# Entry of the attention's heads around two gate tiles, a second accumulator for the modulation, and the scan's last squares inside an output tile

## The chip, the core and the metric

One core of a Trainium2 chip runs one program: two blocks of a model at batch 1, 512 tokens, width 1024. TensorE multiplies matrices into PSUM (eight banks of 128 x 512 fp32 values), VectorE (DVE) and ScalarE (ACT) do elementwise work and functions, GpSimd (POOL) does elementwise work in SBUF, and SyncE (SP) issues DMAs. Every engine works through its own list of instructions in order and waits on semaphores. The metric is the time of one execution in microseconds; lower is better.

## What is computed

The stretch that the change touches lies in the first block. Cut to what matters:

```
mod = silu(c) @ w_ada + b_ada                    # six pieces of 1024: shift1, scale1, gate1, shift2, ...
h = rms_norm(x, norm1_w) * (1 + scale1) + shift1
q, k, v, xBC, z, dt_raw, gates = split(h @ w_in)
q, k = rms_norm per head, then axial rope
attn = softmax(q k^T / 8) v                      # 16 heads of 64, 4 kv heads, not causal
ssd = rms_norm((scan forward + scan backward + D x) * silu(z), ssd_norm_w)
merged = sigmoid(gates_a) * (attn @ w_attn_out) + sigmoid(gates_s) * (ssd @ w_ssd_out)
x = x + gate1 * (merged @ w_o)
```

All products are fp32 accurate. The second block (a recurrent layer and a latent attention) follows unchanged.

## The kernel before

**Tiles.** Activations lie feature by token, 512 tokens wide. A feature tile (`feature_tile`, L1032) is 128 output features: for each of 8 input blocks (4 for an output tile of the scan, `so`) three matmuls of 512 columns, high x high, high x low and low x high part, all into one PSUM bank; 24 matmuls (L1028 to L1030). With `mid=` a function is called on TensorE after half of the blocks.

**Weights.** They stream as 459 slabs of four blocks in the order of `plan()` (L105), two slabs for a tile of 8 blocks. SP loads a slab into one of 4 `w_raw` buffers, ScalarE copies the high part into one of 7 `w_hi` buffers (L592), GpSimd subtracts for `w_lo` (L550). `hi_upto(s)` stands in ScalarE's list wherever the conversion of slabs up to s is to be done, `AHEAD` = 6 slabs ahead of the tile in hand. A w_raw buffer is refilled once its w_lo is done, a w_hi buffer once the tile using it is done. GpSimd also does the rotary products of tile j (`rotate`, L540 and L541) at a fixed slab, seven behind the tile's own.

**Banks.** Each tile has a PSUM bank by its place in the order (L190 to L197): scan tiles from banks 0, 1, 7, the q, k, v tiles and late early-gate tiles from 0 and 1. It starts when the bank's last user has been read. Banks 0 and 1 serve the heads too: `ROW` (row of the negated maxima) is bank 0, `OQ` banks 7 and 1, `PST` (norm sums and statistics) and `OT` bank 2, `M` 3 and 4, `S` 5 and 6, `ADA` 7.

**End of the scan.** After the 16th pair TensorE does `stat("ssd", 15)` (L1195): four matmuls of one column over `sq_sum`, which holds the sum of earlier squares, then four over the last square from ScalarE. Then the last 8 output tiles, `("so", 3, m)`; block k of these needs `bL` of pair 12 + k.

**Projections.** Tiles k0, q0, k1, four value tiles, q1 to q7. A tile's statistic (`qk_stat`, one matmul of 512 columns) stands in the middle of the next tile. ScalarE: square, copy to `t[j % 2]` (L724) once tile j-2 is roped, root (`qk_root`, L734). VectorE per tile: shuffle (L1736), reciprocal of 512 columns (L1746), sum (L1741), product (L1775). Six tiles `("ga", m)` of the attention gate are done early, ScalarE taking their tanh into `gates_early` (L637): ga4 comes after q6, ga5 after q7.

**Heads.** For each head: two-part scores (L1241, L1242) of four key chunks alternate with the next head's scores for the maxima (L1221); VectorE takes the maxima (L1809), TensorE turns them into a row (`row_of_max`, L1229), ScalarE writes this into the 65th row of `q_lo` (L755), so that scores come out less their maximum; exponentials (L770); probabilities x values (L1250). Head 0's own maxima have no head to hide in: scores for maxima (0,0) and (0,1) follow q5, (0,2) and (0,3) follow ga4. After ga5 TensorE waits until all v tiles, q6, q7, ga4 and ga5 are evacuated, then does head 0's row, the q7 statistic and head 0.

**Modulation.** The 24 weight pieces of `w_ada` (2048 wide) are multiplied by silu(c) and added on VectorE (`ada_add`), 8 pieces for each third of the result; TensorE sums over partitions (`ada_reduce`: 16 matmuls of one column, L1098), VectorE takes the result (`ada_finish`). Thirds 2 and 3 run in the loop over m that merges gates and projections (tiles ga, gs, wa; two pieces per step), both in one buffer `acc2`. Third 2 is complete at the end of step m = 3 and is reduced after wa of step m = 4; third 3 is reduced amid the `wo` tiles. ScalarE issues the loads of the pieces (L781), each after the addition that frees its buffer; they stand in its list between the w_hi copies.

Of the kernel before, what the change touches and what calls it, by code (L numbers as in the profile page):

```python
# [9 lines left out]
ACT = mybir.ActivationFunctionType  # L10
# [52 lines left out]
EARLY_IN_QK = {("q", QT - 2): 4, ("q", QT - 1): 5}  # L63
# [127 lines left out]
for _name in TILES:  # L191
    _early = _name[0] == "ga" and _name[1] < N_EARLY
    _ring = (0, 1, 7) if _name[0] in MIXER or _early and _name[1] not in EARLY_IN_QK.values() else \
        (0, 1) if _name[0] in NARROW or _early else \
# [38 lines left out]

LAST_TILE = {}
# [20 lines left out]
def build(nc, d):  # L255

    with ExitStack() as ctx:
# [50 lines left out]
        with Arena():  # L308
# [32 lines left out]
            with Arena():  # L341
                cH, cL = sb("c_hi", [P, KT, SEQ], F32R), sb("c_lo", [P, KT, SEQ], F32R)
                piece2 = [sb(f"ada2_piece{b}", [P, ADA_W]) for b in range(2)]
                acc2 = sb("ada2_acc", [P, ADA_W])
# [235 lines left out]
        def _(act):  # L580
# [154 lines left out]

            for n, name in enumerate(QK):
                hi_upto(slab_of(name) + AHEAD)
                if n and n != KVT + 1:
                    qk_root(QK[n - 1])
                qk_copy(name)  # L740
                if name in EARLY_IN_QK:
                    gate_early(("ga", EARLY_IN_QK[name]))
# [10 lines left out]
            def max_row(h):  # L753
                act.wait_ge(rows_done, h + 1)
                A(qL[h % Q_RING][HD:HD + 1, :], ROW[0:1, :], ACT.Copy, scale=-1.0).then_inc(row_ready, 1)  # L755

# [4 lines left out]
            max_row(0)  # L761
            qk_root(QK[-1])
            hi_upto(slab_of(("gs", 0)) + AHEAD)
            for h in range(N_Q):
                for c in range(NCH):
                    n = NCH * h + c
                    act.wait_ge(qk_done, n + 1)
                    if h:
                        act.wait_ge(pv_done, n - NCH + 1)
                    A(PT[:, c, :], S[n % 2][:, :], ACT.Exp, scale=HD ** -0.5).then_inc(exp_done, 1)  # L770
# [236 lines left out]
        def _(pe):  # L1007
# [121 lines left out]
            def mixer_tile(name):  # L1129
# [4 lines left out]
                feature_tile(name, lambda k: bH[:, half + k, :], lambda k: bL[:, half + k, :], (rdyB, PPG * name[1]))  # L1134
# [60 lines left out]
            stat("ssd", PAIRS - 1)  # L1195
            for m in range(KT):
                mixer_tile(("so", N_GROUPS - 1, m))
# [63 lines left out]

            for n, name in enumerate(QK):
                feature_tile(name, in_a, in_a_lo, mid=(lambda: qk_stat(QK[n - 1])) if n and n != KVT + 1 else None)
                if n == 0:
                    rows("ssd")
                if n == KVT:
                    value_tiles()
                if name == ("q", QT - 3):
                    pe.wait_ge(y_ev, PAIRS)
                    for i in range(2):  # L1270
                        scores_for_max(0, i)
                if name in EARLY_IN_QK:
                    feature_tile(("ga", EARLY_IN_QK[name]), in_a, in_a_lo)
                if name == ("q", QT - 2):
                    for i in range(2, NCH):
                        scores_for_max(0, i)
# [1009 lines left out]
```

## Time and profile before

| | us |
|---|---|
| median of 3 runs | 1741.84 |
| lowest, highest run | 1740.32, 1755.98 |
| profiled execution | 1750.95 |
| its span, first to last instruction | 1749.2 |
| TensorE busy in the span | 1653.6 |
| VectorE, ScalarE, GpSimd busy | 1016.8, 743.0, 777.1 |
| mean granted TensorE clock | 0.969 |

The page of the profile gives busy time per engine, the chain of work that ended last, and groups of instructions by source line. TensorE's busy time includes the pipelined ends of its matmuls, so that it says little about small gaps; the timeline's idle times say more. The granted clock is 1.00 at 2.4 GHz and 0.50 at 1.2 GHz.

### The profile page before, as it was taken

What the parts mean: (1) busy time and instruction counts of PE and PEld (TensorE: products, weight loads), DVE (VectorE), ACT (ScalarE), POOL (GpSimd) and SP (SyncE); (2) the same over time, 40 slices, a digit from 0 to 9 for tenths busy, and PEclk for the clock granted to TensorE, in tenths of its full rate; (3) what the DMA queues carried; (4) which work ended last, traced back from release to release, by engine and by line L of the source; (5) the groups of instructions that cost most, each with busy time, mean ns of one, the idle gap of its engine ahead of it and who ended that gap; (6) DMA issues with size and microseconds to landing.
All of it is one profiled execution on the core that took longest, in us unless ns stands there. A gap on an engine that the chain in (4) does not pass through costs nothing.

```text
span 1749.2 us, 24032 instructions
## 1 busy us (share of the span) xinstructions
PE 1653.6 (95%) x8428; PEld 1365.8 (78%) x8428; DVE 1016.8 (58%) x1357; ACT 743.0 (42%) x1351; POOL 777.1 (44%) x548
## 2 busy tenths in 40 slices
PE   4899999999999899989989999999998799899998
PEld 4678888888787688878868888888887687677776
DVE  4778988988549497576241312122588624357652
ACT  2366655666434444222242323234566344323322
POOL 1245555656546310356534444445534363234433
PEclk9999999999999899989999999999999899799998
DMA  7243344334322100476323333333322232111211
GB/s 297 61 133 106 109 121 133 116 107 117 104 83 73 48 25 1 139 245 232 107 73 99 94 103 91 102 92 96 93 82 79 78 101 75 42 49 55 61 35 68
DMA packets 76390, 171.58 MB, mean 98 GB/s; under 512 B 8256, under 2 KB 8640, under 8 KB 72960
## 3 DMA queue, kind: packets, MB, share of 16 engines
q1 hardware_dynamic: 69120, 133.62, 25.9%
q10 hardware_dynamic: 7168, 36.57, 5.9%
q8 instruction: 68, 1.11, 0.3%
q14 instruction: 34, 0.28, 0.1%
HBM read 167.93 MB, written 2.23 MB: 97 GB/s over the span
## 4 chain that ended last, share of the span: by engine, by line
PE 80%; DVE 12%; ACT 3%; issue 2%; DMA 1%; POOL 0%; SPq 0%; DVEq 0%; ACTq 0%; POOLq 0%
PE bank L1028 21%; PE bank L1030 21%; PE bank L1029 21%; PE bank L1250 3%; DVE rstd L1746 1%; PE bank L1060 1%; PE bank L1430 1%; PE bank L1098 1%; PE bank L1184 1%; DMA x_stream<-x 1%; PE bank L1241 1%; DVE tmp L1593 1%; PE bank L1242 1%; PE bank L1192 1%; PE bank L1221 1%
## 5 line engine op out<-in xcount | busy, mean ns | idle before, releaser
L550 POOL TENSOR_TENSOR w_lo<-w_raw,w_hi 128x512 fp32r<-128x512 f32 x459 | 685.2, 1514 | 696.4 <-ACT w_hi L592 696.3
L1028 PE MATMUL bank<-a_hi,w_hi 128*128 128x512 f32 x1040 | 418.7, 403 | 16.6 <-DVE a_lo L1532 7.9
L1029 PE MATMUL bank<-a_lo,w_hi 128*128 128x512 f32 x1040 | 408.6, 393 | 0.0
L1030 PE MATMUL bank<-a_hi,w_lo 128*128 128x512 f32 x1040 | 408.3, 393 | 0.0
L592 ACT ACTIVATE w_hi<-w_raw 128x512 fp32r<-128x512 f32 x459 | 263.1, 620 | 161.9 <-PE bank L1030 137.6
L1028 PEld LDWEIGHTS bank<-a_hi,w_hi 128*128 128x128 f32 x1040 | 197.2, 190 | 68.4 <-issue 15.6
L1028 PE MATMUL bank<-b_hi,w_hi 128*128 128x512 f32 x600 | 237.9, 396 | 0.6 <-POOL w_lo L550 0.6
L1030 PE MATMUL bank<-b_hi,w_lo 128*128 128x512 f32 x600 | 236.0, 393 | 0.0
L1029 PE MATMUL bank<-b_lo,w_hi 128*128 128x512 f32 x600 | 235.9, 393 | 0.0
L1030 PEld LDWEIGHTS bank<-a_hi,w_lo 128*128 128x128 f32 x1040 | 197.4, 190 | 42.6
L1029 PEld LDWEIGHTS bank<-a_lo,w_hi 128*128 128x128 f32 x1040 | 197.8, 190 | 41.0 <-issue 1.9
L1028 PEld LDWEIGHTS bank<-b_hi,w_hi 128*128 128x128 f32 x600 | 114.4, 191 | 24.7 <-POOL w_lo L550 1.0
L1030 PEld LDWEIGHTS bank<-b_hi,w_lo 128*128 128x128 f32 x600 | 114.0, 190 | 24.6
L1029 PEld LDWEIGHTS bank<-b_lo,w_hi 128*128 128x128 f32 x600 | 114.2, 190 | 23.7
L1917 DVE SCALAR_TENSOR_TENSOR x_stream<-bank,small,x_stream 128x512 f32<-128x512 f32 x32 | 24.0, 751 | 140.4 <-PE bank L1030 140.4
L1910 DVE TENSOR_TENSOR tmp<-tmp 128x512 f32<-128x512 f32 x32 | 22.7, 708 | 123.5 <-ACT tmp L819 123.5
L690 ACT ACTIVATE M<-cs_rows,cs 128x128 f32<-128x128 f32 x256 | 78.0, 389 | 0.0
L1593 DVE SCALAR_TENSOR_TENSOR tmp<-bank,small,tmp 128x510 f32<-128x510 f32 (+1 forms) x96 | 72.0, 750 | 3.4
L504 POOL TENSOR_TENSOR square_sum<-square_sum,sq 128x512 f32<-128x512 f32 x31 | 40.1, 1292 | 64.6 <-ACT sq L604 64.6
L1508 DVE SCALAR_TENSOR_TENSOR ada_acc<-ada_piece,small,ada_acc 128x2048 f32<-128x2048 f32 x21 | 61.9, 2948 | 7.9 <-DMA ada_piece<-ada 6.1
L1250 PEld LDWEIGHTS bank<-v_and_ones,probs 128*128 128x128 f32 x512 | 63.7, 201 | 0.9
L1250 PE MATMUL bank<-v_and_ones,probs 128*128 128x65 f32 x512 | 63.8, 280 | 0.0
(328 smaller groups left out, 2500.9 us busy)
## 6 DMA issues: line engine op xcount, KB each, us to landing
w_raw<-ws SPq DMA_DIRECT2D x459, 256.0 KB, 2.7
cs_rows<-cs_scratch ACTq DMA_DIRECT2D x16, 1024.0 KB, 5.2
ada_piece<-ada ACTq DMA_DIRECT2D x16, 1024.0 KB, 5.7
ada_piece<-ada SPq DMA_DIRECT2D x8, 1024.0 KB, 14.9
x_stream<-x SPq DMA_DIRECT2D x1, 2048.0 KB, 16.2
x_stream<-x ACTq DMA_DIRECT2D x1, 2048.0 KB, 8.4
out<-x_stream SPq DMA_DIRECT2D x8, 256.0 KB, 2.2
rope_table<-rope ACTq DMA_DIRECT2D x1, 512.0 KB, 4.4
```

Of the source, the lines that this page charges most:

```text
L504: nc.gpsimd.tensor_tensor(sq_sum[:, :], first[:, :], sq[n % 2][:, :], ALU.add).then_inc(sq_added, 1)
L550: nc.gpsimd.tensor_tensor(wlo[b][:, :], raw[n % RAW_RING][:, :], r32(whi[b][:, :]), ALU.subtract)\
L592: A(whi[n % RING][:, :], raw[n % RAW_RING][:, :], ACT.Copy).then_inc(hi_done, 1)
L690: a(A(Dm[:, r, w], csB[:, r, w], ACT.Abs, bias=csT[:, c, h:h + 1]))
L1028: mm(out, lh, rh, start=first, stop=False)
L1029: mm(out, lh, rl, start=False, stop=False)
L1030: return mm(out, ll, rh, start=False, stop=last)
L1250: ins = mm(OQ[h % 2][:, i * W:(i + 1) * W], PT[:, c, i * P:(i + 1) * P], vv[:, c, h // 4, :], start=(c == 0 and i == 0), stop=(c == NCH - ...
L1508: V.scalar_tensor_tensor(into[:, :], src[:, :], csl[:, k:k + 1], into[:, :], ALU.mult, ALU.add).then_inc(ada_acc, 1)
L1593: ins = V.scalar_tensor_tensor(out[:, o], src[:, s], cwh[:, j * 24 + i:j * 24 + i + 1], out[:, o], ALU.mult, ALU.add)
L1910: v(V.tensor_tensor(full[:, :], r[:, :], r[:, :], ALU.mult))
L1917: inc_evac(V.scalar_tensor_tensor(xF[:, m, :], gb(name)[:, :], modc[:, 5 * KT + m:5 * KT + m + 1], xF[:, m, :], ALU.mult, ALU.add), name)
```

## The change

- The statistic of the scan's last squares is called in the middle of the first of the last 8 output tiles instead of ahead of it.
- ga4 follows q5 instead of q6, with the q5 statistic in its middle; q6 has none. The order of weights and the rotations' slabs follow. By the rule for banks ga4 and q7 are in bank 1 and q6 in bank 0; ga5 is put into bank 1.
- Scores for head 0's maxima (0,2) and (0,3) follow q6. The row of head 0's maxima is done in the middle of q7, after the q6 statistic, once q6 is evacuated (bank 0). VectorE takes these two maxima ahead of q6's shuffle.
- Before head 0 TensorE waits for the last v tile only. The q7 statistic and tile ga5 stand between scores (0,1) and (0,2); the waits for q7 and ga5 stand after head 0's scores. ScalarE has ga5's tanh and the w_hi copies up to gs0's slabs ahead of exponential (0,2).
- `acc2` becomes two buffers; the second third is reduced after wa of step m = 6, and VectorE takes its result at the end of that step.

```diff
-EARLY_IN_QK = {("q", QT - 2): 4, ("q", QT - 1): 5}
+EARLY_IN_QK = {("q", QT - 3): 4, ("q", QT - 1): 5}
...
+        (1,) if _name == ("ga", N_EARLY - 1) else (0, 1) if _name[0] in NARROW or _early else \
...
+LAST_IN_BANK0 = [n for n in TILES if BANK_OF[n][0] == 0 and n in QK_AT or n == ("ga", N_EARLY - 2) and BANK_OF[n][0] == 0][-1]
...
-                acc2 = sb("ada2_acc", [P, ADA_W])
+                acc2 = [sb(f"ada2_acc{b}", [P, ADA_W]) for b in range(2)]
...
             for n, name in enumerate(QK):
                 hi_upto(slab_of(name) + AHEAD)
-                if n and n != KVT + 1:
+                if n and n != KVT + 1 and QK[n - 1] not in EARLY_IN_QK:
                     qk_root(QK[n - 1])
+                if n + 1 == len(QK):
+                    max_row(0)
                 qk_copy(name)
-                if name in EARLY_IN_QK:
+                if name == ("q", QT - 3):
+                    hi_upto(slab_of(("ga", EARLY_IN_QK[name])) + AHEAD)
+                    qk_root(name)
                     gate_early(("ga", EARLY_IN_QK[name]))
...
-            max_row(0)
             qk_root(QK[-1])
-            hi_upto(slab_of(("gs", 0)) + AHEAD)
...
+                    if (h, c) == (0, 2):
+                        gate_early(("ga", EARLY_IN_QK[QK[-1]]))
+                        hi_upto(slab_of(("gs", 0)) + AHEAD)
                     A(PT[:, c, :], S[n % 2][:, :], ACT.Exp, scale=HD ** -0.5).then_inc(exp_done, 1)
...
-            stat("ssd", PAIRS - 1)
             for m in range(KT):
-                mixer_tile(("so", N_GROUPS - 1, m))
+                mixer_tile(("so", N_GROUPS - 1, m), mid=(lambda: stat("ssd", PAIRS - 1)) if m == 0 else None)
...
+            def middle_of(n):
+                if n and n != KVT + 1 and QK[n - 1] not in EARLY_IN_QK:
+                    qk_stat(QK[n - 1])
+                if n + 1 == len(QK):
+                    wait_evac(pe, LAST_IN_BANK0)
+                    row_of_max(0)
...
+                if name in (("q", QT - 3), ("q", QT - 2)):
+                    if name[1] == QT - 3:
+                        pe.wait_ge(y_ev, PAIRS)
+                    for i in range(2):
+                        scores_for_max(0, 2 * (name[1] - (QT - 3)) + i)
                 if name == ("q", QT - 3):
-                    pe.wait_ge(y_ev, PAIRS)
-                    for i in range(2):
-                        scores_for_max(0, i)
-                if name in EARLY_IN_QK:
-                    feature_tile(("ga", EARLY_IN_QK[name]), in_a, in_a_lo)
-                if name == ("q", QT - 2):
-                    for i in range(2, NCH):
-                        scores_for_max(0, i)
-            for name in [("v", c) for c in range(NCH)] + QK[-2:] + [("ga", m) for m in EARLY_IN_QK.values()]:
-                wait_evac(pe, name)
-            row_of_max(0)
-            qk_stat(QK[-1])
+                    feature_tile(("ga", EARLY_IN_QK[name]), in_a, in_a_lo, mid=lambda: qk_stat(name))
+            wait_evac(pe, ("v", NCH - 1))
             for h in range(N_Q):
                 for c in range(NCH):
                     scores(h, c)
+                    if (h, c) == (0, 1):
+                        qk_stat(QK[-1])
+                        feature_tile(("ga", EARLY_IN_QK[QK[-1]]), in_a, in_a_lo)
                     if h + 1 < N_Q:
                         scores_for_max(h + 1, c)
+                if h == 0:
+                    wait_evac(pe, QK[-1])
+                    wait_evac(pe, ("ga", EARLY_IN_QK[QK[-1]]))
...
-                if m == KT // 2:
+                if m == KT - 2:
                     pe.wait_ge(o_ev, N_Q)
-                    ada_reduce(acc2, 1)
+                    ada_reduce(acc2[0], 1)
...
-                    ada_reduce(acc2, 2)
+                    ada_reduce(acc2[1], 2)
...
                 if k == 0:
-                    if p:
-                        ve.wait_ge(ada_red, p // KT)
...
-            swap_halves(QK[-2])
             for i in range(2, NCH):
                 max_of(0, i)
+            swap_halves(QK[-2])
...
-                if m == KT // 2:
+                for p in (KT + 2 * m, KT + 2 * m + 1):
+                    ada_add(p, acc2[p // KT - 1])
+                if m == KT - 2:
                     ada_finish(1)
-                for p in (KT + 2 * m, KT + 2 * m + 1):
-                    ada_add(p, acc2)
```

## Rows read from the trace of the kernel before

**Rows 1.** The page: the chain that ended last, and ScalarE's w_hi copies.

```profile
PE 80%; DVE 12%; ACT 3%; issue 2%; DMA 1%; POOL 0%; SPq 0%; DVEq 0%; ACTq 0%; POOLq 0%
...
L592 ACT ACTIVATE w_hi<-w_raw 128x512 fp32r<-128x512 f32 x459 | 263.1, 620 | 161.9 <-PE bank L1030 137.6
```

**Rows 2.** Timeline, TensorE, scan's end: start, duration, instruction, [idle before it <-releaser].

```profile
468.77 1.05 PE L1060 MATMUL bank<-consts,square_sum 128*128 128x1 f32 x8
471.69 1.05 PE L1060 MATMUL bank<-consts,sq 128*128 128x1 f32 x8 [1.87 <-ACT sq L604]
472.61 0.49 PE L1028 MATMUL bank<-b_hi,w_hi 128*128 128x512 f32 x1
...
477.05 0.40 PE L1028 MATMUL bank<-b_hi,w_hi 128*128 128x512 f32 x1
```

**Rows 3.** Timeline, TensorE, entry of the heads to head 2.

```profile
571.89 1.10 PE L1221 MATMUL bank<-k_hi_over_lo,q_hi_twice 128*128 128x512 f32 x2 [0.46 <-DVE small L1809]
...
575.57 1.02 PE L1082 MATMUL bank<-sq,consts 128*128 128x512 f32 x2
...
589.41 1.08 PE L1229 MATMUL bank<-consts,small 128*128 128x128 f32 x4 [3.94 <-ACT gates_early L637]
...
606.27 0.77 PE L1241 MATMUL bank<-q_hi_twice,k_hi_over_lo 128*128 128x512 f32 x1
...
610.68 1.89 PE L1250 MATMUL bank<-v_and_ones,probs 128*128 128x65 f32 x16
...
614.56 0.48 PE L1241 MATMUL bank<-q_hi_twice,k_hi_over_lo 128*128 128x512 f32 x1
```

**Rows 4.** Busy time by stretch: PE, PEld, DVE, ACT, POOL, then granted clock, DMA.

```profile
125.00:130.00 5.00, 2.86 (x13) 2.05 (x11) 4.90 (x13) 4.39 (x10) 0.69 (x1) 1.00 0.47 168
130.00:135.00 5.00, 4.72 (x65) 4.36 (x66) 2.79 (x6) 0.23 (x1) 1.97 (x1) 1.00 0.51 170
...
600.00:605.00 5.00, 5.00 (x26) 5.00 (x26) 1.34 (x3) 0.59 (x1) 0.00 (x0) 0.50 0.00 0
```

**Rows 5.** Timeline, TensorE: first matmuls of tiles, and both sums of the modulation.

```profile
757.12 0.39 PE L1028 MATMUL bank<-a_hi,w_hi 128*128 128x512 f32 x1
...
762.56 0.39 PE L1028 MATMUL bank<-b_hi,w_hi 128*128 128x512 f32 x1
...
772.67 6.24 PE L1098 MATMUL bank<-consts,ada_acc 128*128 128x1 f32 x32 [4.51 <-issue]
...
786.64 0.39 PE L1028 MATMUL bank<-b_hi,w_hi 128*128 128x512 f32 x1
...
852.21 3.94 PE L1098 MATMUL bank<-consts,ada_acc 128*128 128x1 f32 x32
...
864.47 0.39 PE L1028 MATMUL bank<-c_hi,w_hi 128*128 128x512 f32 x1
```

**Rows 6.** Timeline, VectorE, q5's product and head 0's last two maxima.

```profile
577.00 0.69 DVE L1775 TENSOR_TENSOR q_full<-tmp,rstd 128x512 f32<-128x512 f32 x1
...
578.36 1.27 DVE L1809 TENSOR_REDUCE small<-bank 128x1 f32<-128x512 f32 x2
```

**Rows 7.** Timeline, ScalarE: table loads, and the tanh of ga4.

```profile
62.27 1.28 ACT L633 ACT_TABLE_LOAD   x1 [5.94 <-DVE tmp L1593]
...
573.20 1.28 ACT L637 ACT_TABLE_LOAD   x1
574.50 0.60 ACT L637 ACTIVATE gates_early<-bank 128x512 f32<-128x512 f32 x1
...
579.87 1.28 ACT L734 ACT_TABLE_LOAD   x1
...
594.17 1.28 ACT L770 ACT_TABLE_LOAD   x1
```

**Rows 8.** Timeline, VectorE and GpSimd: additions of step m = 4, a pair of w_lo.

```profile
779.24 2.11 DVE L1505 TENSOR_SCALAR ada_acc<-ada_piece,small 128x2048 f32<-128x2048 f32 x1
781.47 3.17 DVE L1508 SCALAR_TENSOR_TENSOR ada_acc<-ada_piece,small,ada_acc 128x2048 f32<-128x2048 f32 x1
...
774.23 2.96 POOL L550 TENSOR_TENSOR w_lo<-w_raw,w_hi 128x512 fp32r<-128x512 f32 x2 [3.81 <-ACT w_hi L592]
```

More of the change, by code:

```diff
@@ L193 @@
     _ring = (0, 1, 7) if _name[0] in MIXER or _early and _name[1] not in EARLY_IN_QK.values() else \
-        (0, 1) if _name[0] in NARROW or _early else \
+        (1,) if _name == ("ga", N_EARLY - 1) else (0, 1) if _name[0] in NARROW or _early else \
         (0, 1, 2) if _name[0] in LATENT else (0, 1, 3, 4, 5, 6)
@@ L734, in qk_root, with max_row @@
                 A(out[:, :], PST[:, :], ACT.Sqrt, bias=eps).then_inc(qk_std, 1)
+            def max_row(h):
+                act.wait_ge(rows_done, h + 1)
+                A(qL[h % Q_RING][HD:HD + 1, :], ROW[0:1, :], ACT.Copy, scale=-1.0).then_inc(row_ready, 1)
             for n, name in enumerate(QK):
                 hi_upto(slab_of(name) + AHEAD)
-                if n and n != KVT + 1:
+                if n and n != KVT + 1 and QK[n - 1] not in EARLY_IN_QK:
                     qk_root(QK[n - 1])
+                if n + 1 == len(QK):
+                    max_row(0)
                 qk_copy(name)
-                if name in EARLY_IN_QK:
+                if name == ("q", QT - 3):
+                    hi_upto(slab_of(("ga", EARLY_IN_QK[name])) + AHEAD)
+                    qk_root(name)
                     gate_early(("ga", EARLY_IN_QK[name]))
@@ L751, in _ @@
                                    ACT.Copy), ("v", c))
-            def max_row(h):
-                act.wait_ge(rows_done, h + 1)
-                A(qL[h % Q_RING][HD:HD + 1, :], ROW[0:1, :], ACT.Copy, scale=-1.0).then_inc(row_ready, 1)
             def round_pair(u):
@@ L1127, in _, with mixer_tile @@
             pe.wait_ge(tot_e, 1)
-            def mixer_tile(name):
+            def mixer_tile(name, mid=None):
                 if name[0] != "so":
@@ L1133, in mixer_tile @@
                 half = name[1] % 2 * PPG
-                feature_tile(name, lambda k: bH[:, half + k, :], lambda k: bL[:, half + k, :], (rdyB, PPG * name[1]))
+                feature_tile(name, lambda k: bH[:, half + k, :], lambda k: bL[:, half + k, :], (rdyB, PPG * name[1]), mid)
             for i in range(PAIRS):
@@ L1260, in turn_pair @@
                 ins.then_inc(turned, 1)
+            def middle_of(n):
[4 more added lines that the diff above has]
+                    row_of_max(0)
             for n, name in enumerate(QK):
-                feature_tile(name, in_a, in_a_lo, mid=(lambda: qk_stat(QK[n - 1])) if n and n != KVT + 1 else None)
+                feature_tile(name, in_a, in_a_lo, mid=lambda: middle_of(n))
                 if n == 0:
```

## The prediction

> **What bounds the kernel.** I read the page first: the chain of work that ended last runs through TensorE for 80% of the span [rows 1]. VectorE holds 12%, in the scan, the q/k norms and a few joints. So an edit pays where TensorE stands still or where its clock is down; elsewhere it moves slack. TensorE's waits, and then its timeline, show three places inside the stretch that the diff touches:
>
> - End of the scan: the first sum for the ssd norm (L1060) starts at 468.77, the second waits 1.87 us for a square, the first output tile starts at 472.61, the next only at 477.05 [rows 2].
> - Entry of the heads: 3.94 us of idle before the row of maxima (L1229) at 589.41, and head 1's scores start at 606.27 [rows 3]; the granted clock is 0.50 in 600 to 605 [rows 4].
> - The modulation: 4.51 us of idle before the sum at 772.67 [rows 5].
>
> The clock is the second thing to read. A tile of 24 matmuls takes 762.56 - 757.12 = 5.44 us [rows 5], 0.227 us a matmul, with 1.00 granted, the 2.4 GHz level. At 0.50, which is 1.2 GHz, it is nearly twice that: the first output tile's twelve take 477.05 - 472.61 = 4.44 us instead of 2.72 [rows 2].
>
> **Scan's last squares.** The same 16 column sums are issued, but behind six matmuls. Before: 468.77 to 477.05 [rows 2]. After: six matmuls, 1.36, bring TensorE to 470.1; the first sum, 0.9 by the second one's 472.61 - 471.69, to 471.0; the square still comes at 471.69; the second sum ends at 472.6, the other six matmuls at 474.0 at full clock. The tile's last block needs b_lo of pair 15, made from the same x_feat as that square and not asked for before 473.3. Gain 477.05 - 474.0 = 3.1 us. If the clock falls again as before, the same 1.7 us (4.44 - 2.72) are lost: 1.4. I take 3.1, since 0.7 us of idle stays of 1.87. The q/k chain on VectorE starts from TensorE's tile k0 and moves along.
>
> **Entry of the heads.** Tile ga4 goes from behind q6 to behind q5. All tiles up to the scores for maxima (0,2) are the same in number, so these scores stay at 571.89, where they wait 0.46 us for VectorE's first maximum already [rows 3]. Then comes q7. Its middle is at 575.57 as now; the q6 statistic ends at 576.4 (two slots of 0.43 at the clock's full level, with its weights). New there is the row of maxima. It needs maxima (0,2) and (0,3): VectorE ends q5's product at 577.69, and two maxima take 1.27 [rows 6]; swap_halves(q6), now ahead of them, goes behind. So they end at 579.0, and TensorE waits 579.1 - 576.4 = 2.7 us in the middle of q7: **a new wait**, with q7's second half, the scores and ga5 queued behind it. With 0.45 for the transposes and 2.8 for twelve matmuls, q7 ends at 582.4.
>
> ScalarE must by then have written the maxima into q_lo. It converts w_hi of slabs 151 and 152, which hang on DMAs and those on POOL, as now; loads the Sqrt table at 579.87, 1.28 [rows 7]; does the root and the row, 0.6 each like its neighbours: 582.4, just in time. Scores (0,0), maxima scores (1,0), scores (0,1) are five matmuls: 583.6. The q7 statistic, 0.86: 584.5. ga5, 5.44: 589.9. Its weights are there, for POOL now stops for q6's rotation before slab 151 and no longer before 149. The root of q7, the Exp table and the first two exponentials lie under ga5 on ScalarE. Seven more matmuls: 591.5. Now TensorE waits for ga5's evacuation: ScalarE was held until scores (0,2), done at 590.8, and has two w_hi (620 ns each [rows 1]) ahead of the tanh of 0.60 [rows 7]: 592.6, 1.0 us, **the second new wait**. Four groups of value matmuls with the next row of maxima take 614.56 - 610.68 = 3.9 [rows 3]: head 1 starts at 596.5. The two w_hi behind the tanh and exponentials (0,2) and (0,3) end at 594.7, before they are needed at 594.8.
>
> Before, head 1 starts at 606.27, and its twelve matmuls take 610.68 - 606.27 = 4.4 [rows 3] instead of 2.8. Gain 606.27 - 596.5 + 1.6 = 11.3. Upper bound 12: VectorE's maxima can't come earlier. Lower bound 8: a fall of the clock after the 2.7 us can cost what follows the second modulation sum (3 us, below), and 0.3 for a late w_hi.
>
> A rule of the Trainium skill (ScalarE: Activation LUTs, "Table sets: the hidden batching unit") says that Exp and Tanh share a table set, so that a Tanh among exponentials needs no load. The trace agrees: none follows the one at 62.27 in the whole scan, where both run. There are five loads from 573.20 to 594.17 [rows 7], and by this rule three in the new order (Tanh, Sqrt, Exp). The page's "What ACT_TABLE_LOAD costs" puts a switch at about 2.66 us with its drain; here the next instruction starts 574.50 - 573.20 = 1.30 us after the load. By the page's price the late root would come 1.4 us later and the gain be an estimated 9.9; by the row it is 11.3, and the row decides.
>
> **Modulation.** TensorE ends wa4 at 762.56 + 5.44 = 768.0, waits, sums, and ends the next tile at 786.64 [rows 5]: 18.64 us with 5.44 of tile in it, price 13.2. The second sum, without a wait, goes from 852.21 to 864.47 with its next tile: 12.26 - 5.5, price 6.8, of which 3.9 are the sum [rows 5] and 3 half clock behind it. After the change the first sum stands behind wa6, at about 796; its last addition has ended when the sum starts at 772.67 now. No wait, price 6.8. Gain 6.4.
>
> But TensorE comes sooner to gs5 to wa6, and the supply of weights hangs on VectorE: ScalarE issues the next ada loads, and does the w_hi behind them, only once the additions are done. In step m=4 these start at 779.24 and take 2.11 and then 3.17 [rows 8], to 784.6, as before (the sum's result before them is 0.2). Then tanh 0.6, w_hi 0.6, POOL 1.5 (half of 2.96 [rows 8]) and gaps of some 0.4: slab 177 is ready at 787.7. TensorE, if it never stalled, would want it at 787.0: 0.7 us of **new wait**. Slab 179 is ready at 792.6 and wanted at 793.2. Gain 6.4 - 0.7 = 5.7. Bounds: 6.4, and 3.9 if slabs 177 and 179 come 0.9 us later each. The second accumulator itself takes no time; it removes a wait of VectorE's that had always ended. The wo tiles need c_lo of m=7, which VectorE has about 0.8 us before it is asked for.
>
> **Sum.** 3.1 + 11.3 + 5.7 = 20.1 us. The profiled execution took 1750.95, so the changed one should take 1730.9. The three timed runs have a median of 1741.84, 9.1 lower than the profiled run, so I forecast 1741.84 - 20.1 = 1721.7. What comes later is in the same order and moves as a whole.
>
> **Rivals.**
> 1. The clock falls at one of the two joints that remain (2.7 us in q7, or the sums in the output tile). For: 1.87 us of idle between two sums was enough at 472 [rows 2]. Against: over 2.1 us without work in 125 to 130, between dense matmuls, left it at 1.00 there and in the next window [rows 4]. Price 1.7 to 3: 1724. The Trainium skill (TensorE: Matmul & The Clock Gate, "The HAM clock gate") says that throttled is the default and activity releases it; which way 2.7 us go, that does not say.
> 2. The weights take the modulation's gain: gs6 and wa6 wait for w_lo. For: margins of 0.6 us. Against: each step stands in rows. Gain 14: 1728.
> 3. The entry gains half: the maxima in q_lo and ga5's tanh are each 2 us late through ScalarE's queue, and VectorE, with less reserve in heads 2 to 8, gives back 2 more. Gain 14 or less: 1728 to 1733.
> 4. Slower: the clock falls in q7, and the mixed work of the heads does not raise it. A head at half clock costs up to 6.3 us more (3.9 doubled, and 4.4 to 5.2 for 2.8). From the fourth such head the 20 us are gone, from the sixth or seventh it is over 1% slower; with eight, 1772. Against: it rose within head 1 last time, after worse idling [rows 3].
>
> **Chances.** Forecast 0.47, rival 1 0.25, rival 2 0.11, rival 3 0.13, rival 4 0.04. One per cent is 17.4 us, about what a measurement of this kernel can tell from no change; the line is at 1724.4. The forecast lies below it nine times in ten (0.42), rival 1 half the time (0.13), the others within, but for three of rival 4's four parts: faster 0.55, same 0.42, slower 0.03. The bounds give 1741.84 - 21.5 = 1720.3 and 1741.84 - 13.3 = 1728.5. The executions scatter by more (1740.32 to 1755.98), and rival 3 reaches 1733: range 1714 to 1733.
>
> **What would show it.** In the changed profile: under 1 us of idle before the second L1060 sum of the scan, and three steps of output tiles without a slow one; an idle of 2.5 to 3 us before the transposes of the maxima in the middle of q7, released by VectorE's maxima; ga5 between scores (0,1) and (0,2), with 1 us on gates_early soon after; granted clock 1.00 from there; head 1's scores some 13 us earlier; no idle before the first L1098 after the attention, and at most 1 us on w_lo in gs6. It is wrong if the clock is down in heads 0 and 1, if more than 3 us are waited for w_lo between 750 and 790, or if TensorE waits for VectorE in heads 2 to 8.

## The result: 1733.1 us, and the profile after

| | before | after |
|---|---|---|
| median | 1754.57 (1740.32 to 1755.98, five runs) | 1733.12 (1724.17 to 1734.71, five runs) |
| ratio | | 0.9895, interval 0.9854 to 0.9936 |
| profiled execution, its span | 1750.95, 1749.2 | 1734.71, 1732.9 |
| granted clock, mean | 0.969 | 0.975 |

The change makes the kernel 1.05% faster; in two later comparisons the ratio was 0.9896 and 0.9893. The prediction was 1721.7 us and the range ended at 1733, so the median came 11.4 us above the forecast. Of these, 9.1 are the time that the sum was subtracted from. The sum was too large as well: the span of the profiled execution shrank by 16.3 us where it said 20.1.

In these five runs each, both kernels' times lie in two groups: before near 1741 and near 1755, after near 1724 and near 1734. If the lower group of one answers to the lower group of the other, which isn't shown, the change is worth 17 and 21 us.

The first view is TensorE's timeline of the changed kernel at the end of the scan. It answers to [rows 2]. Columns: start, duration, instruction, count, and in brackets the idle time before and who ended it.

```profile
469.42 0.50 PE L1034 MATMUL bank<-b_hi,w_hi 128*128 128x512 f32 x1
...
470.93 0.95 PE L1066 MATMUL bank<-consts,square_sum 128*128 128x1 f32 x8
472.34 1.05 PE L1066 MATMUL bank<-consts,sq 128*128 128x1 f32 x8 [0.47 <-ACT sq L605]
473.26 0.48 PE L1034 MATMUL bank<-b_hi,w_hi 128*128 128x512 f32 x1
...
474.08 0.63 PE L1034 MATMUL bank<-b_hi,w_hi 128*128 128x512 f32 x1
...
477.44 0.39 PE L1036 MATMUL bank<-b_hi,w_lo 128*128 128x512 f32 x1
```

Six matmuls of the output tile now run ahead of the sums, and the wait for the last square is 0.47 us instead of 1.87. But from 474.08 to 477.07 the matmuls start 0.43 us apart instead of 0.227: half clock, about 1.6 us of it. The windows say the same:

```profile
470.00:475.00 5.00, 4.53 (x27) 3.90 (x26) 1.73 (x3) 2.28 (x4) 2.11 (x2) 0.90 0.00 0
475.00:480.00 5.00, 5.00 (x19) 4.04 (x18) 1.38 (x2) 1.26 (x2) 3.89 (x7) 0.76 0.39 105
580.00:585.00 5.00, 5.00 (x16) 3.88 (x16) 0.02 (x1) 2.51 (x5) 4.91 (x4) 0.68 0.28 61
585.00:590.00 5.00, 5.00 (x21) 3.76 (x20) 0.67 (x1) 3.51 (x5) 0.00 (x0) 1.00 0.36 100
```

(Busy time of PE, PEld, DVE, ACT, POOL, then the granted clock, as in [rows 4]. The two lower ones belong to the next view.)

TensorE's timeline at the entry of the heads, which answers to [rows 3]:

```profile
571.07 1.10 PE L1226 MATMUL bank<-k_hi_over_lo,q_hi_twice 128*128 128x512 f32 x2 [0.39 <-DVE small L1823]
...
574.74 1.02 PE L1088 MATMUL bank<-sq,consts 128*128 128x512 f32 x2
579.27 0.62 PE L1234 MATMUL bank<-consts,small 128*128 128x128 f32 x4 [3.52 <-DVE small L1823]
579.65 0.67 PE L1034 MATMUL bank<-a_hi,w_hi 128*128 128x512 f32 x1
580.12 0.63 PE L1035 MATMUL bank<-a_lo,w_hi 128*128 128x512 f32 x1
...
583.38 0.39 PE L1034 MATMUL bank<-a_hi,w_hi 128*128 128x512 f32 x1
...
584.08 0.39 PE L1246 MATMUL bank<-q_hi_twice,k_hi_over_lo 128*128 128x512 f32 x1
...
585.25 1.02 PE L1088 MATMUL bank<-sq,consts 128*128 128x512 f32 x2
585.70 0.80 PE L1034 MATMUL bank<-a_hi,w_hi 128*128 128x512 f32 x1
```

The new wait stands where it was foreseen, in the middle of q7, released by VectorE's maxima; it is 3.52 us, not 2.7, and q7's second half starts at half clock (0.68 in 580 to 585). ga5 follows at full clock; its tanh is waited for 0.83 us at 594.23, and head 1 starts at 598.18. Why the maxima were late shows in VectorE's timeline and in GpSimd's beside it:

```profile
574.91 1.23 DVE L1755 TENSOR_TENSOR tmp<-tmp 128x512 f32<-128x512 f32 x1
576.17 1.63 DVE L1789 TENSOR_TENSOR q_full<-tmp,rstd 128x512 f32<-128x512 f32 x1
577.84 1.29 DVE L1823 TENSOR_REDUCE small<-bank 128x1 f32<-128x512 f32 x2
...
573.05 5.87 POOL L551 TENSOR_TENSOR w_lo<-w_raw,w_hi 128x512 fp32r<-128x512 f32 x4
```

From the trace of the kernel before, GpSimd's timeline at the same place, and the same product for all eight q tiles (shortest, median and longest in ns, first and last start):

```profile
573.89 2.53 POOL L550 TENSOR_TENSOR w_lo<-w_raw,w_hi 128x512 fp32r<-128x512 f32 x2
...
L1775 DVE TENSOR_TENSOR q_full<-tmp,rstd x8: 691/1656/1668, 522.4 to 661.4; 128x512 f32<-128x512 f32 x8
```

q5's product took 0.69 us before [rows 6], and GpSimd had ended its pair of w_lo blocks at 576.42, ahead of the product's start at 577.00. Now GpSimd makes four w_lo blocks from 573.05 to 578.92, all around it. The price could have been read ahead of the change: the median of this product was 1.66 us in the kernel before, and the 0.69 of [rows 6] was its shortest. A rule of the Trainium skill (SBUF — State Buffer, "Who interferes with whom") says that a VectorE instruction with two inputs in SBUF contends with a GpSimd instruction that reads SBUF, and that one of them blocks. This product has two such inputs, and the trace agrees that it takes longer there: 1.63 us beside w_lo, 0.69 us alone. Which engine blocked, and for how long at a time, it doesn't tell. The maxima behind it read PSUM and kept their 1.29.

ScalarE's table loads, which answer to [rows 7]:

```profile
567.52 1.28 ACT L638 ACT_TABLE_LOAD   x1
...
579.23 1.28 ACT L735 ACT_TABLE_LOAD   x1
580.53 0.69 ACT L735 ACTIVATE std<-bank,small 128x512 f32<-128x512 f32 x1
...
587.01 1.28 ACT L776 ACT_TABLE_LOAD   x1
```

There are three loads, as the rule of the Trainium skill (ScalarE: Activation LUTs, "Table sets: the hidden batching unit") gave in the prediction. The root starts 1.30 us after its load's start, as the row of before had it, and not after the 2.66 us of the Trainium skill (ScalarE: Activation LUTs, "What ACT_TABLE_LOAD costs"); the measurement decides.

TensorE's timeline in the modulation, which answers to [rows 5]:

```profile
778.13 0.50 PE L1034 MATMUL bank<-a_hi,w_hi 128*128 128x512 f32 x1 [0.52 <-POOL w_lo L551]
...
786.43 3.63 PE L1104 MATMUL bank<-consts,ada_acc 128*128 128x1 f32 x32
789.92 0.48 PE L1034 MATMUL bank<-a_hi,w_hi 128*128 128x512 f32 x1
...
791.37 0.60 PE L1034 MATMUL bank<-a_hi,w_hi 128*128 128x512 f32 x1
...
797.09 0.39 PE L1034 MATMUL bank<-a_hi,w_hi 128*128 128x512 f32 x1
...
813.39 0.51 PE L1034 MATMUL bank<-c_hi,w_hi 128*128 128x512 f32 x1 [0.43 <-DVE c_lo L1885]
...
836.19 4.09 PE L1104 MATMUL bank<-consts,ada_acc 128*128 128x1 f32 x32
840.13 0.77 PE L1034 MATMUL bank<-c_hi,w_hi 128*128 128x512 f32 x1
```

The 4.51 us ahead of the first sum are gone. Two small waits have come: 0.52 us for w_lo in gs6, foreseen, and 0.43 us for c_lo in the second wo tile, not foreseen. All in all the joint at w_lo costs 0.8 us: gs6 takes 6.26 us instead of 5.44.

Behind the first sum, from 786.43 to the end of the next tile at 797.09, TensorE takes 10.66 us, 5.2 more than the tile alone. In a second execution of the same kernel it took 9.02, 3.6 more, since the clock didn't fall there. The windows 790 to 795 of the first and the second execution:

```profile
790.00:795.00 5.00, 5.00 (x16) 3.97 (x16) 3.97 (x4) 1.97 (x4) 5.00 (x4) 0.66 0.77 264
...
790.00:795.00 5.00, 5.00 (x28) 4.33 (x28) 3.08 (x3) 2.89 (x6) 4.08 (x3) 1.00 0.90 320
```

**Where the time went, by stages.** The three places, and the stages beside them that the diff leaves alone, can be cut at TensorE instructions that wait in all kernels (the square's sum; the x_stream wait of k0; the first scores for maxima (0,2); the transposes behind the last head; the n2 roots). Length of each stretch in us:

| stretch | before | before, 2nd profile | after | after, 2nd | after, 3rd |
|---|---|---|---|---|---|
| scan, up to the last square | 290.88 | 290.91 | 290.79 | 290.92 | 290.84 |
| scan's end | 25.37 | 25.36 | 23.97 | 24.02 | 23.95 |
| k and q tiles | 74.83 | 74.79 | 74.76 | 74.75 | 74.76 |
| attention | 141.19 | 140.83 | 132.40 | 132.38 | 132.39 |
| modulation | 165.91 | 166.60 | 159.50 | 156.69 | 157.17 |
| second block: latent attention, three stretches together | 205.78 | 205.78 | 205.53 | 205.34 | 198.62 |
| span | 1749.2 | 1751.2 | 1732.9 | 1730.6 | 1725.3 |

The first profile of each gives 1.4 + 8.8 + 6.4 = 16.6. With the means it is 1.4 + 8.6 + 8.5 = 18.5 us, 1.06% of 1750. That is near the measured 1.05%, but the modulation's stretch alone spreads over 2.8 us in three executions of one kernel, so the agreement proves little.

### The profile page after: what moved, and what is told of

The parts are those of the page before. It is cut to its first block and busy times, and to the rows that moved or that the text cites. A ratio compares the mean times of both kernels' runs of the same rounds, so it can differ in the third digit from the quotient of the medians.

```text
span 1732.9 us, 24027 instructions
## 1 busy us (share of the span) xinstructions
PE 1643.7 (95%) x8428; PEld 1357.0 (78%) x8428; DVE 1017.7 (59%) x1357; ACT 740.0 (43%) x1349; POOL 779.3 (45%) x548
## 5 line engine op out<-in xcount | busy, mean ns | idle before, releaser
L825 ACT ACTIVATE tmp<-bank 128x512 f32<-128x512 f32 x32 | 19.1, 598 | 101.3 <-PE bank L1036 101.3
L1255 PEld LDWEIGHTS bank<-v_and_ones,probs 128*128 128x128 f32 x512 | 60.2, 192 | 1.9 <-ACT gates_early L638 1.2
## 6 DMA issues: line engine op xcount, KB each, us to landing
x_stream<-x SPq DMA_DIRECT2D x1, 2048.0 KB, 16.6
```

What stands on the lines that cost most here:

```text
L1255: ins = mm(OQ[h % 2][:, i * W:(i + 1) * W], PT[:, c, i * P:(i + 1) * P], vv[:, c, h // 4, :], start=(c == 0 and i == 0), stop=(c == NCH - ...
```

## Experiments

**One part at a time.** Three kernels, each with one of the three parts alone, and the changed kernel again.

The scan's part alone:

```diff
-            stat("ssd", PAIRS - 1)
             for m in range(KT):
-                mixer_tile(("so", N_GROUPS - 1, m))
+                mixer_tile(("so", N_GROUPS - 1, m), mid=(lambda: stat("ssd", PAIRS - 1)) if m == 0 else None)
```

> The kernel before with the scan's last squares alone inside the output tile. Reading of the two traces: the wait shrinks from 1.87 to 0.47 us, but the clock falls all the same, so the part gives about 1.5 us. The step of the prediction (clock stays up) would give 3.1 us. A rival, that the two traces differ by scatter alone here, would give 0.

Measured: 1752.9 us (before 1753.16), ratio 0.9993, interval 0.9949 to 1.0038. By times alone nothing can be told from no change. The stretch of the scan's end tells it: 23.97 us against 25.37, 1.4 less, with the same fall of the clock behind the second sum (seven matmuls at 0.43 us). The 3.1 of the forecast didn't come, and the trace speaks against the rival of scatter alone: in the table this stretch repeats to 0.1 us for each kernel.

The entry alone (the change with the scan's and the modulation's parts undone):

```diff
+            stat("ssd", PAIRS - 1)
...
-                mixer_tile(("so", N_GROUPS - 1, m), mid=(lambda: stat("ssd", PAIRS - 1)) if m == 0 else None)
+                mixer_tile(("so", N_GROUPS - 1, m))
...
-                acc2 = [sb(f"ada2_acc{b}", [P, ADA_W]) for b in range(2)]
+                acc2 = sb("ada2_acc", [P, ADA_W])
...
```

> The changed kernel with the scan's squares and the modulation as before: the entry of the heads alone. If the parts add, it gives 8.9 us by the traces (11.3 was predicted), with a wait of about 3.5 us in the middle of q7, q5's product on VectorE (L1789 of the changed kernel) at 1.6 us beside GpSimd, and half clock behind the wait. If the wait in q7 were 0.9 us shorter because the stretch starts at another time, the product would take 0.7 us.

Measured: 1738.18, ratio 0.9947 (0.9918 to 0.9976); attention 133.46 against 141.19, 7.7 less where 8.9 were expected. The wait in q7, from TensorE's timeline of this kernel, is the same to the hundredth:

```profile
584.98 1.09 PE L1235 MATMUL bank<-consts,small 128*128 128x128 f32 x4 [3.52 <-DVE small L1826]
```

Here the half clock behind it lasted eleven matmuls instead of eight, and took in more of the transposes: from the transposes to head 0's first scores it is 5.89 us instead of 4.81, which is the 1 us to the changed kernel's 132.4. How long the clock stays down behind the same wait thus differs from execution to execution.

The modulation alone:

```diff
-                acc2 = sb("ada2_acc", [P, ADA_W])
+                acc2 = [sb(f"ada2_acc{b}", [P, ADA_W]) for b in range(2)]
...
-                if m == KT // 2:
+                if m == KT - 2:
...
-                    ada_reduce(acc2, 1)
+                    ada_reduce(acc2[0], 1)
...
```

> The kernel before with the modulation's part alone. If the parts add: 6.4 us by the traces (5.7 was predicted), with waits of 0.5 us on w_lo and 0.4 us on c_lo that the kernel before does not have. If the modulation's gain hung on the earlier entry, it would be under 4 us.

Measured: 1738.78, ratio 0.9925 (0.9899 to 0.9952); modulation 156.68 against 165.9 to 166.6, and the two new waits are there without the rest of the change: 0.48 us for w_lo, 0.86 us for c_lo. So both come from this part, and they don't depend on the attention's coming earlier. The stretch is 9.2 us shorter than in the first profile of the kernel before, where 6.4 were expected. The difference is the clock: behind the first sum it stayed at 1.00 in this execution. Over all eight profiles with the two sums as the change has them, it fell behind the second sum in eight and behind the first in six; where it didn't fall behind the first (this one and the second of the changed kernel) the stretch is 156.7 us, in the others 157.2 to 160.4.

> The changed kernel itself, on the same chip as its parts. If the parts add, its gain over the kernel before is their sum, 16 to 17 us. If executions fall into two groups for both kernels, this run and the kernel before show the same group in the same round.

Measured: 1732.8, ratio 0.9896 (0.9844 to 0.9948); stretches in the table. The parts alone give 1.4, 7.7 and 9.2 us, 18.3 together, against 16.6 to 18.5 in the whole: they add up within the scatter of the modulation. Whether two kernels are in the same group in the same round, these times don't show.

**What made the maxima late.** GpSimd's w_lo is held back until VectorE has done q5's product:

```diff
+HOLD_AT = slab_of(("q", QT - 1)) + 3
...
+                    if n == HOLD_AT:
+                        pool.wait_ge(rope_done, QK_AT[("q", QT - 3)] + 1)
```

> The changed kernel, but GpSimd does w_lo of slab 149 only after q5's product. Theory: the product L1789 took 1.63 us instead of 0.69 because GpSimd worked beside it; it will take 0.7, the maxima come 0.9 us sooner, and the wait in q7 is 2.6 us instead of 3.5. Rival: the product's length comes from something else and stays 1.6. Second question: if 2.6 us of idle are short enough for the clock, the half clock behind the wait goes as well (stretch of the attention 132.4 to 129.9 us); if not, it stays (131.5).

Measured: 1733.97, ratio 0.9888 (0.9859 to 0.9917). VectorE's timeline, then TensorE's, of this kernel:

```profile
575.84 0.69 DVE L1794 TENSOR_TENSOR q_full<-tmp,rstd 128x512 f32<-128x512 f32 x1
576.56 1.29 DVE L1828 TENSOR_REDUCE small<-bank 128x1 f32<-128x512 f32 x2
...
578.00 0.62 PE L1239 MATMUL bank<-consts,small 128*128 128x128 f32 x4 [2.55 <-DVE small L1828]
```

The product is back at 0.69 us, the wait at 2.55, near the 2.7 that was predicted, and the attention's stretch is 0.9 us shorter (131.49). So GpSimd was the cause of this 0.9. And the clock fell all the same for seven matmuls behind 2.55 us of idle; the predicted wait is longer than this, so it would most likely have lost the clock too.

**What lets the clock fall at the end of the scan.** The pooled sum stays in the first output tile, the last square's goes into the second:

```diff
-                mixer_tile(("so", N_GROUPS - 1, m), mid=(lambda: stat("ssd", PAIRS - 1)) if m == 0 else None)
+                mixer_tile(("so", N_GROUPS - 1, m), mid={0: lambda: pooled_squares("ssd"), 1: lambda: last_square("ssd", PAIRS - 1)}.get(m))
```

> The changed kernel with the two sums of the scan's squares in two different output tiles (the sum of the pooled squares in the first, the last square's in the second). Theory: the two runs of one-column matmuls with the gap between them let the clock fall; apart they don't, and the last stretch of the scan takes 2.2 us less than in the changed kernel (0.5 idle, 1.7 clock). Rival: the clock falls after the scan's own small matmuls whatever stands behind; then 0.5 us.

Measured: 1735.51, ratio 0.9897 (0.9858 to 0.9936). TensorE's timeline of this kernel:

```profile
474.17 0.95 PE L1066 MATMUL bank<-consts,square_sum 128*128 128x1 f32 x8
474.98 0.47 PE L1034 MATMUL bank<-b_hi,w_hi 128*128 128x512 f32 x1
...
478.04 0.95 PE L1066 MATMUL bank<-consts,sq 128*128 128x1 f32 x8
478.85 0.48 PE L1034 MATMUL bank<-b_hi,w_hi 128*128 128x512 f32 x1
```

No wait and no slow step: from the first output tile (472.66) to the x_stream wait (497.57) it is 24.91 us, against 496.31 - 469.42 = 26.89 in the changed kernel. 2.0 us less, the 1.6 of half clock and the wait. The edit takes away two things at once, the 0.47 us of idle and the nearness of the two sums, and no run parts them; the theory speaks of both together. In all eleven profiles with the two sums in one place the clock fell behind them, in the three with the sums apart it didn't. The total doesn't show it, because in this profiled execution the scan itself took 1.7 us more, where the two kernels have the same instructions.

**What the two other sums cost.** Each of the sixteen columns of the two late modulation sums is put behind one block of a tile:

```diff
+            def ada_column(src, j, b):
+                if b == 0:
+                    pe.wait_ge(ada_acc, KT * (j + 1))
+                    pe.wait_ge(mod_ready, j)
+                ins = mm(ADA[:, b:b + 1], src[:, b * P:(b + 1) * P], ones[:, 0:1], start=True, stop=True)
...
-                feature_tile(("gs", m), in_a, in_a_lo)
+                feature_tile(("gs", m), in_a, in_a_lo, each=(lambda k: ada_column(acc2[0], 1, k)) if here else None)
...
```

> The changed kernel with each of the two later modulation sums spread, one of its 16 matmuls behind each block of two tiles (gs6 and wa6, wo3 and wo4). Theory: what costs beside the sum's own 3.6 us is the half clock that a run of one-column matmuls leaves behind (1.6 and 3 us); spread, it goes, and the stretch between attention and second norm takes 4 to 5 us less. Rival: a one-column matmul among dense ones costs more than 0.23 us each, and the gain is under 2 us.

Measured: 1729.08, ratio 0.986 (0.9832 to 0.9889); modulation 155.10. That is 4.4 us less than in the first profile of the changed kernel, but 1.6 less than in its second, where the first sum left no half clock behind. From TensorE's timeline, two of the sixteen, and the wait that grew:

```profile
779.80 0.28 PE L1114 MATMUL bank<-consts,ada_acc 128*128 128x1 f32 x2
780.72 0.28 PE L1114 MATMUL bank<-consts,ada_acc 128*128 128x1 f32 x2
...
816.56 0.50 PE L1034 MATMUL bank<-c_hi,w_hi 128*128 128x512 f32 x1 [1.41 <-DVE c_lo L1897]
```

A block of three matmuls comes every 0.92 us instead of 0.68; the two tiles take 7.26 and 7.36 us instead of 5.44, so a sum costs 3.7 us (3.5 in one piece), but no half clock follows. What is won there is partly lost again: c_lo is waited for 1.41 us, because TensorE comes sooner.

**Without the wait in q7.** The row of maxima stands behind q7, and the first scores, the second head's first scores for maxima and q7's statistic stand inside ga5, whose tanh goes ahead of ScalarE's wait for scores:

```diff
-        (1,) if _name == ("ga", N_EARLY - 1) else ...
+        (7,) if _name == ("ga", N_EARLY - 1) else ...
...
+                    if (h, c) == (0, 2):
+                        gate_early(("ga", EARLY_IN_QK[QK[-1]]))
...
-                if n + 1 == len(QK):
-                    wait_evac(pe, LAST_IN_BANK0)
-                    row_of_max(0)
...
+            wait_evac(pe, LAST_IN_BANK0)
+            row_of_max(0)
...
+            feature_tile(("ga", EARLY_IN_QK[QK[-1]]), in_a, in_a_lo, mid=first_scores)
...
```

> The changed kernel with the row of head 0's maxima behind q7 instead of in its middle, the scores (0,0), (0,1), maxima scores (1,0) and the q7 statistic in the middle of ga5 (which has bank 7), and ga5's tanh ahead of ScalarE's wait for scores (0,2). Theory: the wait of 3.5 us in q7 is a matter of place; behind q7 only 0.8 us of it stay, the clock stays up, and head 0's values start 4.8 us sooner (attention 127.6 us instead of 132.4). Rival: the wait turns up again, on the row in q_lo or on ga5's evacuation, and under 2 us are gained.

Measured: 1720.93 (1719.95 to 1721.91), ratio 0.9814 (0.9785 to 0.9842); attention 127.58, 4.8 less than the changed kernel. TensorE's timeline and two windows:

```profile
580.81 0.62 PE L1234 MATMUL bank<-consts,small 128*128 128x128 f32 x4 [0.79 <-DVE small L1827]
...
575.00:580.00 5.00, 5.00 (x21) 3.45 (x19) 4.90 (x5) 0.75 (x2) 5.00 (x4) 1.00 0.37 107
580.00:585.00 5.00, 4.21 (x22) 3.54 (x22) 1.38 (x5) 4.36 (x6) 4.04 (x4) 1.00 0.38 103
```

0.79 us of idle instead of 3.52, and the granted clock stays at 1.00. The maxima are no earlier; TensorE has the twelve matmuls of q7's second half to do before it needs them. The total flatters this kernel: its later latent attention took 195.5 us in the profiled execution, 10 less than in the first profile of the changed kernel, with the same instructions.

**Together, and how sure the total is.** All four edits; the same without the spread sums; the changed kernel; and a second profile of the kernel before. The edits are the four diffs above.

> The changed kernel with the scan's sum of squares in two halves in two output tiles, the two last modulation sums one matmul per block of tiles, the row of maxima behind the last latent query tile with the first scores inside the early gate tile, and the sums on GpSimd held back until VectorE's product behind the last but one latent query tile is done. Mechanisms add up: the scan's end 2.0 us less than in the changed kernel (no half clock behind it), the attention stretch 4.8 less for the row and 0.9 for the held sums (132.4 to about 126.7), the modulation stretch about 1.6 less: 8.5 to 9.5 us in all, so about 1723.5 beside 1733 in executions of the same kind. Rival 1 (the gains compete for the same reserve of clock, so that it falls elsewhere instead): 1728 or more. Rival 2 (the modulation's spread only moves the stall to the weights of wa6): its stretch is no shorter than 159, and the total 1725 to 1726.

Measured: 1718.5 (1712.95 to 1725.57), ratio 0.9824 (0.9782 to 0.9867). From the last wait of the scan to the x_stream wait 312.83 us (314.76 in the changed kernel), attention 126.98, modulation 157.27. Scan and attention did what was expected, 1.9 and 5.4 less. The modulation didn't come out 1.6 below the changed kernel's 156.7 to 159.5. Two things stand against it: the wait for c_lo, and a half clock right behind the last head, where the kernel with the spread sums alone had 1.00. From TensorE's timeline and the windows:

```profile
695.00:700.00 5.00, 4.27 (x18) 3.54 (x18) 1.30 (x3) 0.60 (x1) 0.00 (x0) 0.67 0.27 70
...
807.03 0.50 PE L1039 MATMUL bank<-c_hi,w_hi 128*128 128x512 f32 x1 [1.66 <-DVE c_lo L1914]
```

Beside the 155.10 us of the spread sums alone this execution has 2.2 us more. The half clock at its start is 1.6 of them (the first tile ends 7.6 us after the stretch's start instead of 6.0), c_lo only 0.25, since 1.41 were waited for there too. Behind the sums themselves the clock stayed up. Whether that half clock comes from the four edits together (the first rival) or from the execution is open: one profile shows it, and the kernel with three of the edits doesn't. The totals of both rivals (1725 and more) didn't come.

> As the kernel with all four edits, but with the modulation's sums left as the change has them. It tells what the spread sums are worth beside the others: if they are worth 1.6 us, this one stands at about 1725 and its modulation stretch at 157 to 160; if the spread only traded the half clock for slower tiles, the two kernels do not differ, at about 1724. The scan's end and the attention stretch (about 126.7) are the same in both.

Measured: 1727.57 (1718.82 to 1730.09), ratio 0.9874 (0.983 to 0.9917); 312.85, 127.20 and 160.36. Beside the kernel with all four the modulation's stretch is 3.1 us longer, and the half clock is back: the granted clock is 0.55 in 785 to 790 and 0.72 in 835 to 845, where it is 1.00 with the spread sums. That the spread takes the half clock away is shown, in both kernels that have it and behind both sums. What it is worth is not one number: 156.7 to 160.4 us without, 155.1 and 157.3 with it.

> The changed kernel again, for the ratio to the kernel before with more rounds. By the sum of the stages (16.3 us of 1751) the ratio is 0.9905 within executions of the same kind; by the prediction's sum of 20.1 us it would be 0.9885. Rival: the change also keeps the clock up in the later latent attention, and then the ratio is below 0.988 and the stage table of this execution differs from that of the kernel before there.

Measured: 1728.11 (1723.21 to 1734.11), ratio 0.9893 (0.985 to 0.9937). The ratio lies between the two that were named, 0.9905 and 0.9885, and its interval holds both, so the total doesn't decide between the sums. The rival's sign, a shorter latent attention, is there in this one execution (198.6 against 205.5 and 205.3 in the two others of the same kernel), so the change doesn't bring it each time; whether it makes it more frequent is open.

> The kernel before once more, for a second profile of it. If the two groups of its times (about 1741 and 1755) come from the clock in stages that the change does not touch, this execution has the same attention stretch (141.2) and the same end of the scan (25.4) as the first, and what differs in its span lies in the scan's recurrence or in the later latent attention (27.9 / 19.0 / 158.9 us in the first for its three stretches). If they come from the entry or from the modulation's sums, those stretches differ.

Measured: 1753.01, span 1751.2. The stretches are near those of the first profile (table), the modulation within 0.7 us, the latent attention the same. Both profiles of the kernel before are thus of the upper group, and no profile of the lower was to be had. What is shown: with unchanged instructions, the second block's latent attention took 205.3 to 205.8 us in ten of the fourteen profiles of all kernels, and 201.4, 198.6, 198.4 and 195.5 in the other four. Windows of the changed kernel's first and third profile, 1485 to 1525:

```profile
1485.00:1525.00 40.00, 36.37 (x138) 28.87 (x137) 13.41 (x20) 10.33 (x20) 11.03 (x10) 0.75 0.19 53
...
1485.00:1525.00 40.00, 35.94 (x165) 28.35 (x165) 17.56 (x26) 9.44 (x18) 11.70 (x10) 0.91 0.16 47
```

The same kernel was granted 0.75 in one and 0.91 in the other. That this is the whole distance of 14 us between the groups is open.

## Why the prediction was right or wrong

- **What bounds the kernel**: right. TensorE's idle time and its clock in three places carried the gain of the profiled span, and the two stretches of the first block that the diff leaves alone agree to 0.15 us in the table. (In three kernels of the experiments, among them the entry alone, the scan took 1.7 us more with the same instructions.)
- **Scan's last squares**: 3.1 predicted, 1.4 measured. The order of events came as worked out (0.47 of idle where 0.7 was expected). "I take 3.1, since 0.7 us of idle stays of 1.87" is the mis-sized term: less idle was taken to mean no fall of the clock. It fell in every profile that has the two sums in one place, with 1.87 or 0.47 us between them, and in none with the two in different tiles. That was rival 1, and the stated lower price of 1.4.
- **Entry**: 11.3 predicted, 8.8 measured. The new wait, its place and releaser, the second one behind ga5 (0.83 for 1.0) and the table loads were right. Two terms were short. The product on VectorE was costed at its 0.69 of [rows 6] though the change moved q6's rotation on GpSimd behind slab 150, so that w_lo lay beside it: 0.9. And the clock fell in q7: 1.6. The prediction had put this on the chance that a gap between dense matmuls does no harm, as in [rows 4], where the timeline of before has 2.42 us in one piece; 2.55 us of idle were enough here.
- **Modulation**: 5.7 predicted, 6.4 measured in the first profile, 8.5 by the mean. The idle went as said, w_lo cost 0.8 (0.7 predicted). That the total is so near in the first profile is in part luck. The first sum and what follows it cost 5.2 in one execution and 3.6 in another, where 6.8 were taken from the second sum; c_lo, costed as ready 0.8 us before it is asked for, came 0.4 to 0.9 us late in three profiles of the change's sums, and wasn't waited for in the five others.
- **Sum**: the step that failed most is "The three timed runs have a median of 1741.84, 9.1 lower than the profiled run, so I forecast 1741.84 - 20.1". Three executions out of two groups, 14 us apart, had two in the lower one; with two more, the median of the five is 1754.57, and the later sets had 1753.16, 1753.68 and 1752.23. From the profiled execution's own 1750.95, to which every row belongs, the same sum gives 1730.9, 2.2 below the measured median and 3.8 below the profiled execution of the changed kernel. The two medians of the result differ by 21.5 us, near the sum's 20.1, but that doesn't bear the sum out: its terms measured 1.4, 8.8 and 6.4. The range of 1714 to 1733 was laid around the wrong centre: the scatter was named, but used for its upper end only as far as rival 3 reached.
- **Chances**: 0.55 for faster by over 1%, and the ratio of 0.9895 lies right on that line, with an interval on both sides of it. Rival 1 came true at both of its places, the two in one run. Rivals 2, 3 and 4 did not: w_lo cost 0.8 us, q_lo was written at 581.82, ahead of head 0's first scores, and the granted clock is 1.00 from 592 to 703, through all the heads.

## What to carry to other kernels

Subtract a sum made from a trace from the time of the execution that left this trace, and only then ask how that execution stands to the others. When a duration is taken from one row, look at the same instruction's other rows first. When a wait is moved into dense work, count what the clock does behind it as part of its price, and look for enough independent work to put ahead of the wait; twelve matmuls ahead of the wait turned 3.52 us of idle and a slow stretch into 0.79 and none. When a step changes place on GpSimd, look at which VectorE instructions with two SBUF inputs it now lies beside.

## What was unexpected

- **Short joints cost the clock.** The two sums of squares, 0.9 us each, with 0.47 us of idle between them were followed by eight or so matmuls at the 1.2 GHz level. A modulation sum, 3.5 us of such matmuls without any idle, was followed by another such stretch in 14 cases of 16 of the change's sums. One sum of squares at a time between wide matmuls, or one column of the modulation behind each block, was followed by none. In q7 2.55 us of idle lost the clock and 0.79 did not; the gap in [rows 4], 2.42 us, lies between them, in other work, and didn't either.
- **VectorE beside GpSimd.** A product of 128x512 with both inputs in SBUF: 0.69 us alone, 1.63 to 1.67 beside w_lo.
- **The same program, another clock.** In unchanged code the latent attention took 195.5 to 205.8 us, more than half of what this change is worth. Some stretches are steadier: the attention repeated to 0.02 us in three executions of the changed kernel, the scan's end to 0.1. But with the same instructions the attention also took 133.4 in two kernels of the experiments, and the modulation spreads over 3.7 us. With a few executions of each, an edit of 1 or 2 us is told by the waits and the clock at its own place; totals don't tell it, and not every stretch does.
- **The best version.** All four edits together reached 0.9824 of the kernel before, where the change has 0.9893 in the same comparison. The row behind q7 alone had 0.9814, in two executions of another comparison, one of them with the short latent attention, so totals don't rank the two; from the scan's first wait to the n2 roots the kernel with all four is 4.1 us shorter (671.8 against 676.0). What still stands in its way there is c_lo, 1.66 us.
